# Queries of heads 4 to 7 and probabilities of heads 0 to 3 turned by VectorE blocks and a DRAM scratch, in a two-layer attention and retention trunk

## What is computed

```python
h = rms_norm(x, norm_mix_g[0])
q, k, v = split(h @ a_w_qkv, 3)                      # 256 x 1024 each, 8 heads of 128
q = rope(rms_norm(q per head, q_gain)); k = rope(rms_norm(k per head, k_gain))
s = q @ k.T * 128 ** -0.5;  s = where(causal, s, -1e30);  p = softmax(s)
x = x + (p @ v) @ a_w_o
x = x + square(relu(rms_norm(x) @ w1)) @ w2          # layer 0's MLP
x = x + retention_mixer(rms_norm(x));  x = x + mlp(rms_norm(x))
```

## Time and profile before

| | us |
|---|---|
| median of 3 runs | 663.09 (661.23 to 663.13) |
| the profiled execution's own time | 662.9 |
| its span, first to last instruction | 661.1 |
| PE busy | 655.7 (99% of the span) |
| DVE busy | 430.3 (65%) |
| ACT busy | 332.4 (50%) |
| POOL busy | 26.8 (4%) |

### The profile page before, as it was taken

How to read it: one execution, slowest core, us unless ns; L and a number is a source line. 1 busy time by engine, 2 the same in 40 slices (tenths; PEclk the granted TensorE clock), 3 DMA queues, 4 the chain that set the end, 5 groups by cost and what they waited for, 6 DMA issues and landing times.

```text
span 661.1 us, 8673 instructions
## 1 busy us (share of the span) xinstructions
PE 655.7 (99%) x3248; PEld 553.4 (84%) x3248; DVE 430.3 (65%) x481; ACT 332.4 (50%) x435; POOL 26.8 (4%) x29
## 2 busy tenths in 40 slices
PE   8999999999999999999999999999999999999998
PEld 7888888888888888888888888888888888888887
DVE  6798656877776445549984765765588777744531
ACT  7777664655554333454445555554465555533320
POOL 0163000000000000000000000000000000000000
PEclk9999999999999999999999999999999999999999
DMA  9965457766555657554655657649847655565500
GB/s 325 389 220 190 128 152 246 202 188 188 187 189 192 192 192 257 194 183 154 225 192 193 191 161 276 197 149 288 234 148 216 193 193 183 191 208 195 187 1 32
DMA packets 90766, 129.30 MB, mean 196 GB/s; under 512 B 3312, under 2 KB 50928, under 8 KB 90736
## 3 DMA queue, kind: packets, MB, share of 16 engines
q1 hardware_dynamic: 90448, 127.58, 59.6%
q0 software_dynamic: 288, 1.31, 0.5%
HBM read 124.68 MB, written 4.19 MB: 195 GB/s over the span
## 4 chain that ended last, share of the span: by engine, by line
PE 99%; DVE 0%; issue 0%; DVEq 0%
PE acc L635 23%; PE acc L539 19%; PE acc L541 19%; PE acc L540 19%; PE acc L638 11%; PE acc L586 1%; PE acc L583 1%; PE acc L592 1%; PE acc L658 1%; PE scr L541 1%; PE scr L540 1%; PE scr L539 1%; PE scr L671 1%; PE scr L682 1%; PE scr L703 1%; PE scr L766 1%
## 5 line engine op out<-in xcount | busy, mean ns | idle before, releaser
L1046 DVE TENSOR_TENSOR lo<-raw,hi 128x2048 fp32r<-128x2048 f32 x108 | 247.1, 2288 | 109.6 <-ACT hi L806 109.5
L806 ACT ACTIVATE hi<-raw 128x2048 fp32r<-128x2048 f32 x108 | 207.0, 1918 | 139.4 <-PE acc L541 137.4
L635 PE MATMUL acc<-h_both,hi 128*128 128x512 f32 x640 | 224.0, 396 | 0.0
L638 PE MATMUL acc<-h_both,lo 128*128 128x256 f32 x640 | 178.3, 279 | 0.0
L635 PEld LDWEIGHTS acc<-h_both,hi 128*128 128x128 f32 x640 | 120.1, 188 | 28.5
L638 PEld LDWEIGHTS acc<-h_both,lo 128*128 128x128 f32 x640 | 120.5, 188 | 0.0
L539 PE MATMUL acc<-hi,aT_hi 128*128 128x512 f32 x252 | 98.1, 389 | 0.0
L541 PE MATMUL acc<-hi,aT_lo 128*128 128x512 f32 x252 | 98.0, 389 | 0.0
L540 PE MATMUL acc<-lo,aT_hi 128*128 128x512 f32 x252 | 98.0, 389 | 0.0
L539 PE MATMUL acc<-hi,h_both 128*128 128x512 f32 x208 | 83.4, 401 | 0.0
L541 PE MATMUL acc<-hi,h_both 128*128 128x512 f32 x208 | 81.2, 390 | 0.0
(11 more groups left out here) (132 smaller groups left out, 582.5 us busy)
## 6 DMA issues: line engine op xcount, KB each, us to landing
raw<-in_mlp_w SPq DMA_DIRECT2D x64, 1024.0 KB, 5.4
raw<-in_r_w_in SPq DMA_DIRECT2D x24, 1024.0 KB, 5.1
raw<-in_a_w_qkv SPq DMA_DIRECT2D x8, 1024.0 KB, 9.8
raw<-in_r_w_out SPq DMA_DIRECT2D x8, 1024.0 KB, 5.2
raw<-in_a_w_qkv SPq DMA_DIRECT2D x16, 256.0 KB, 6.1
raw<-in_a_w_o SPq DMA_DIRECT2D x4, 1024.0 KB, 5.0
z_rows<-stage_a SPq DMA_DIRECT2D x32, 64.0 KB, 1.8
stage_b<-z_rows SPq DMA_DIRECT2D x8, 256.0 KB, 2.8
```

The lines of the kernel that those rows point to most:

```text
L635: nc.tensor.matmul(bank, feat_view(hi, s)[:, kt, o * P:(o + 1) * P], h_both[:, kt, :, :].rearrange("p b t -> p (b t)"), start=kt == 0, sto ...
L638: m = nc.tensor.matmul(bank[:, 0:SEQ], feat_view(lo, s)[:, kt, o * P:(o + 1) * P], hT_hi[:, kt, :], start=False, stop=kt == KD - 1)
L806: nc.scalar.activation(hi[:, s, :], raw[:, s, :], ACT.Copy).then_inc(hi_ready, 1)
L1046: nc.vector.tensor_tensor(lo[:, s, :], raw[:, s, :], hi[:, s, :].bitcast(F32), ALU.subtract).then_inc(lo_ready, 1)
```

## The change

`T` of groups 4 and 5 and `P` of heads 0 to 3 leave PE and ACT. In their place DVE turns 32x32 blocks: `turn_queries(4)` and `(5)` as a new task `B` at slot 14, into `q_blocks`, and a transpose of 384 columns at the end of `normalised(h)` for h < 4, into `p_blocks`. SP writes the blocks to the DRAM scratches `q_rows` and `p_rows` (four DMAs for each group or head) and reads them back into `qkT` (four DMAs per group, in runs of 32 elements) and `pT` (one per head). `scores(4)` waits for both query reads, `attend(h)` for h < 4 for its read. Its right operand is then read from `pT` in runs of 32. The low part of chunk 9 moves from slot 14 to 15, and that of chunk 10 from 15 to 17. In slots 10 to 19 `left` and `var` now come before `N`.

```diff
-    early = ["scales", "rope", "high", "low", "N", "v", "raw", "left", "var", "T", "A", "P", "S", "E"]
+    early = ["scales", "rope", "high", "low", "left", "var", "N", "B", "v", "raw", "T", "A", "P", "S", "E"]
...
+TURNED = (4, 5)
+STORED = [p for p in range(8) if p not in TURNED]
+TURN_AT = 14
...
-LOW_AT = {1: 3, 3: 4, 5: 7, 7: 9, 9: 11, 11: 13, 13: 14, 17: 18}
+LOW_AT = {1: 3, 3: 4, 5: 7, 7: 9, 9: 11, 11: 13, 13: 15, 15: 17, 17: 18}
...
-            for s, (n, kg) in enumerate(WO_ORDER):
-                load(C_WO // 4, s, tok_view, wo_w[n, kg])
+
+            def write_queries():
+                for t in range(TT):
+                    sp.wait_ge(q_blocks_ready, t + 1)
+                    for i in range(4):
+                        rows = q_rows[t].rearrange("(j r) i c -> i r j c", j=4)[i]
+                        sp.dma_start(rows, q_blocks[32 * i:32 * i + 32, t, :].rearrange("p (j c) -> p j c", j=4)
+                                     ).then_inc(q_out[t], 16)
+
+            def read_queries():
+                for t in range(TT):
+                    sp.wait_ge(q_out[t], 64)
+                    for a in range(4):
+                        sp.dma_start(qkT[:, 0, 4 + a, t * P:(t + 1) * P].rearrange("p (i c) -> p i c", i=4),
+                                     q_rows[t].rearrange("d i (a c) -> a d i c", a=4)[a]).then_inc(q_in[t], 16)
...
+            def read_probs(h):
+                sp.wait_ge(p_out[h], 64)
+                sp.dma_start(pT[:, h, :], p_rows[h].rearrange("d i c -> d (i c)")).then_inc(p_in[h], 16)
...
+            load_wo(0)
+            write_probs(0)
+            write_queries()
+            read_probs(0)
+            write_probs(1)
+            load_wo(1)
+            read_queries()
+            read_probs(1)
+            load_wo(2)
+            write_probs(2)
+            read_probs(2)
+            write_probs(3)
+            load_wo(3)
+            read_probs(3)
...
             def scores(h):
-                pe.wait_ge(qkT_ready, 4 + 4 * (h // 4))
+                pe.wait_ge(qkT_ready, 4 + 2 * (h // 4))
+                if h == 4:
+                    for t in range(TT):
+                        pe.wait_ge(q_in[t], 64)
...
-                pe.wait_ge(pT_ready, h + 1)
+                if h < 4:
+                    pe.wait_ge(p_in[h], 16)
+                    p = pT[:, h, :].rearrange("p (i b c) -> p b i c", i=4, b=3)
+                    first, second = p[:, 0:2], p[:, 2]
+                else:
+                    pe.wait_ge(pT_ready, h - 3)
+                    first, second = pT[:, h % 4, 0:SEQ], pT[:, h % 4, SEQ:384]
...
-                    if what == "T":
+                    if what == "T" and i in STORED:
                         transpose_rot(i)
...
-                    elif what == "P":
+                    elif what == "P" and i >= 4:
                         transpose_p(i)
...
+            def turn_queries(p_i):
+                t = p_i % 2
+                dve.wait_ge(rot_sum_ready, p_i + 1)
+                nc.vector.transpose(q_blocks[:, t, :].rearrange("p (j a c) -> p a j c", j=4, a=4),
+                                    rot[:, t, :].rearrange("p (a j c) -> p a j c", a=4, j=4)
+                                    ).then_inc(q_blocks_ready, 1)
...
+                if h < 4:
+                    dve.wait_ge(p_ready, h + 1)
+                    if h >= 2:
+                        dve.wait_ge(p_out[h - 2], 64)
+                    nc.vector.transpose(p_blocks[:, h % 2, :].rearrange("p (j b c) -> p b j c", j=4, b=3),
+                                        probs[:, h % 3, :].rearrange("p (b j c) -> p b j c", b=3, j=4)
+                                        ).then_inc(p_blocks_ready, 1)
```

More of the change, by code:

```diff
@@ L126, in attention_schedule @@
         at[O_AT[h]].append(("O", h))
+    for p in TURNED:
+        at[TURN_AT].append(("B", p))
     at[SCALES_AT].append(("scales", 0))
     first = ["T", "square", "var", "rope", "factors", "low", "raw", "high", "left"]
-    early = ["scales", "rope", "high", "low", "N", "v", "raw", "left", "var", "T", "A", "P", "S", "E"]
+    early = ["scales", "rope", "high", "low", "left", "var", "N", "B", "v", "raw", "T", "A", "P", "S", "E"]
     late = ["N", "A", "S", "v", "high", "O", "P", "E", "low"]
@@ L181, in program @@
     x_rows = nc.dram_tensor("x_rows", (2, TT, P, 4, P), F32, kind="Internal").ap()
+    q_rows = nc.dram_tensor("q_rows", (TT, P, 4, P), F32, kind="Internal").ap()
+    p_rows = nc.dram_tensor("p_rows", (4, P, 4, 3 * 32), F32, kind="Internal").ap()
     z_rows = nc.dram_tensor("z_rows", (HR, TT, P, 4, P), F32, kind="Internal").ap()
@@ L242, in program @@
         rope_g = at("rope_g", 55 * KB, [P, 2, TT, 2, P])
+        p_blocks = at("p_blocks", 61 * KB, [P, 2, 384])
         mask = at("mask", 59 * KB, [P, 384])
@@ L297, in program @@
         qkT_ready = sem("qkT_ready")
+        q_blocks_ready = sem("q_blocks_ready")
+        q_out = [sem(f"q_out{t}") for t in range(TT)]
+        q_in = [sem(f"q_in{t}") for t in range(TT)]
         v_ready = sem("v_ready")
@@ L304, in program @@
         pT_ready = sem("pT_ready")
+        p_blocks_ready = sem("p_blocks_ready")
+        p_out = [sem(f"p_out{h}") for h in range(4)]
+        p_in = [sem(f"p_in{h}") for h in range(4)]
         o_ready = sem("o_ready")
@@ L424, in _, with write_probs, load_wo @@
                 load_qkv(c)
-            for s, (n, kg) in enumerate(WO_ORDER):
-                load(C_WO // 4, s, tok_view, wo_w[n, kg])
+            def write_queries():
[11 more added lines that the diff above has]
+                                     q_rows[t].rearrange("d i (a c) -> a d i c", a=4)[a]).then_inc(q_in[t], 16)
+            def write_probs(h):
+                sp.wait_ge(p_blocks_ready, h + 1)
+                for i in range(4):
+                    rows = p_rows[h].rearrange("(j r) i c -> i r j c", j=4)[i]
+                    sp.dma_start(rows, p_blocks[32 * i:32 * i + 32, h % 2, :].rearrange("p (j c) -> p j c", j=4)
+                                 ).then_inc(p_out[h], 16)
+            def read_probs(h):
+                sp.wait_ge(p_out[h], 64)
+                sp.dma_start(pT[:, h, :], p_rows[h].rearrange("d i c -> d (i c)")).then_inc(p_in[h], 16)
+            def load_wo(s):
+                load(C_WO // 4, s, tok_view, wo_w[WO_ORDER[s]])
+            load_wo(0)
[12 more added lines that the diff above has]
+            read_probs(3)
             load_w1(0)
@@ L668, in transpose_rot @@
                 if p_i >= 1:
-                    pe.wait_ge(qkT_ready, p_i)
+                    pe.wait_ge(qkT_ready, STORED.index(p_i))
                 for h in range(4):
@@ L686, in transpose_p @@
                 pe.wait_ge(p_ready, h + 1)
-                if h >= 1:
-                    pe.wait_ge(pT_ready, h)
+                if h >= 5:
+                    pe.wait_ge(pT_ready, h - 4)
                 b = scr[:, 1, :]
@@ L702, in attend @@
                 bank = scr[:, BANK_O[h % 2], :]
-                nc.tensor.matmul(bank[:, 0:SEQ], v_att[:, 0, h * P:(h + 1) * P], pT[:, h % 4, 0:SEQ],
+                nc.tensor.matmul(bank[:, 0:SEQ], v_att[:, 0, h * P:(h + 1) * P], first,
                                  start=True, stop=False)
-                nc.tensor.matmul(bank[:, P:SEQ], v_att[:, 1, h * P:(h + 1) * P],
-                                 pT[:, h % 4, SEQ:384], start=False, stop=True).then_inc(o_ready, 1)
+                nc.tensor.matmul(bank[:, P:SEQ], v_att[:, 1, h * P:(h + 1) * P], second,
+                                 start=False, stop=True).then_inc(o_ready, 1)
             def behind(k):
                 for what, i in SCHEDULE[k]:
-                    if what == "T":
+                    if what == "T" and i in STORED:
                         transpose_rot(i)
@@ L898, in store_pT @@
             def store_pT(h):
-                act.wait_ge(pTp_ready, h + 1)
-                if h >= 4:
-                    act.wait_ge(o_ready, h - 3)
+                act.wait_ge(pTp_ready, h - 3)
+                act.wait_ge(o_ready, h - 3)
                 nc.scalar.copy(pT[:, h % 4, :], scr[:, 1, 0:384]).then_inc(pT_ready, 1)
@@ L917, in _ @@
                         norm_squares(0)
-                    elif what == "T":
+                    elif what == "T" and i in STORED:
                         store_qkT(i)
@@ L1145, in rope @@
                     dve.wait_ge(tables_g_ready, 2)
-                if p_i >= 2:
-                    dve.wait_ge(rotT_ready, p_i - 1)
+                if p_i - 2 in TURNED:
+                    dve.wait_ge(q_blocks_ready, p_i - 2 - TURNED[0] + 1)
+                elif p_i >= 2:
+                    dve.wait_ge(rotT_ready, STORED.index(p_i - 2) + 1)
                 sin_done = dv.mark(nc.vector.tensor_tensor(u4, raw4, sin, ALU.mult))
@@ L1179, in masked @@
                 dve.wait_ge(pow_ready, POWER_NO[4 * (h // 4) + 1])
-                if h >= 3:
-                    dve.wait_ge(pTp_ready, h - 2)
+                if 3 <= h < 7:
```

(5 more changed lines are left out.)

5 lines of the change are left out of this document (3 added, 2 removed).

## The result

The changed kernel takes 667.36 us (median of 10 runs, 665.58 to 671.15) against 663.33 for the kernel before beside it: a ratio of 1.0066, 95% interval 1.0049 to 1.0084. It is slower, by some 4.4 us as the ratio has it and 4.0 between the medians, where 1.5 had been forecast. The profiled execution took 669.16 us, its span is 667.4. The trace of after starts 0.25 us later in the work than that of before (the DVE step behind `low` 8 starts at 48.28 and 48.53), so 0.25, its shift, is added to its times where they are set against before's.

What follows compares the result with a forecast made beforehand. PE was taken to bound the kernel, 99% of the chain. 2.20 us won against 3.9 in waits for POOL gave +1.66 on the profiled 662.9, so 664.6 us; range 661.8 to 667.2.

Steps and rivals of the forecast that it cites:

- The ledger of DVE: DVE from `low` 8's end at 48.53: transposes at 0.61 each put `var` 6 at 61.42, `low` 10 at 62.82.
- The collisions: POOL products and DVE steps exclude each other; group 6's meets `low` 10 at 62.8, group 7's meets `low` 11.
- The sum for POOL's wait: PE at `T` 7: starts at 70.1 for 68.11, +2.0 us; less 0.33 for `P` 3, +1.66 to the end.
- scratch trips on SP: SP's DRAM writes and reads, costed at nothing; head 3's read lands at 79 to 80, `attend(3)` asks at 82.1.
- The sign that I had set for it: The forecast is wrong in the step if PE waits at `S` 4 or `attend`.
- the margin as the thinnest of all: Head 3's probability read before `attend(3)` asks for it: 2 us to spare.
- Rival 4: PE after the 3 us wait: TensorE at 1.2 GHz, some 25 matmuls 0.2 slower each, half counted: 667; chance 0.10.
- Short runs in `attend`: PE's right operand in runs of 32: between no cost and 2.6 us over four heads, taken as none.
- Rival 3: Query reads land late, 77.3 against 73.9 when `S` 4 asks, +3.4 us on top: 668; chance 0.08.
- Rivals 1 and 2: 1: PE does not wait, -2.2, 660.9, chance 0.10; 2: DVE's ledger too long, 662 to 663.4, chance 0.14.

Runs made afterwards that it cites:

- the run with both edits: Changed kernel with head 3's read ahead of the fourth output projection load and twelve unused matmuls ahead of the wait at `T` 6: 664.73 us, ratio 1.0031.
- holding the clock: Changed kernel with twelve matmuls whose result nobody reads ahead of the wait at `T` 6: 666.76 us, ratio 1.0062.
- the placed kernel: Changed kernel with `var` 7 a slot sooner, `low` 10, `low` 11 and the high part of chunk 11 a slot later: 667.94 us, ratio 1.0067.
- the last experiment: Changed kernel, `var` 7 sooner, `low` 10, 11 and high 11, 12 later, SP's head 2, 3 writes and reads before both loads: 661.39 us, ratio 1.0002.
- the probabilities alone: Changed kernel with only the probabilities of heads 0 to 3 turned by DVE, queries left on PE: 664.01 us, ratio 1.0016.
- the first run with SP's order mended: Changed kernel, `var` 7 sooner, `low` 10, 11 and high 11, 12 later, reads of heads 2, 3 each ahead of one load: 664.38 us, ratio 1.0024.

## Why the prediction was wrong

- **The ledger of DVE was right.** The wait for head 1's exponential was forecast as 0.9, and is 1.04. `rope` 6 was forecast at 54.49, `var` 6 at 61.42, `low` 10 at 62.82: they are, with the shift, at 54.54, 61.46 and 62.87. The transposes take 0.50 to 0.60 by distance of starts (52.60 to 53.10, and 53.10 to 54.29 for two). The collisions came as worked out, with `low` 10 and the product starting 0.02 us apart. The product for group 7 was to end at 70.0 to 70.1; it ends at 69.89. That the engines take turns so is also the rule of the Trainium skill (SBUF — State Buffer, SBUF: two separate sides, on the shared port pair: whichever starts first has it for the whole instruction). The rows agree that a product and a `low` don't share; which of them goes first the recorded starts don't tell, since the product that starts 0.02 ahead of `low` 10 is the one that waits.
- **The sum for POOL's wait was right to half a microsecond.** With the clock full and the late read out of the way (the run with both edits) `T` 7 starts at 69.90 + 0.50 = 70.4, for 70.1. The rest is a wait that I did not list: `T` 7 needs the copy of `T` 6, and ACT makes the high part of chunk 12 first.
- **The step that failed is "scratch trips on SP", costed at nothing.** I had head 3's read land at 79 to 80, 2 us before `attend(3)` would ask. It landed at 84.7. Three sizes were wrong in it. The query reads, in runs of 128 bytes, take 7.19 us to issue, 0.9 each, where I took 0.44 from the issues of z; that puts the third load at 68.33, for some 64, and head 2's writes right behind it, at 68.80. Those writes landed so late behind it that the next read was issued at 74.62, for 72. And head 3's own read, behind the fourth load, took 6.6 to land, where I took 2.8. The sign that I had set for it, a PE wait at `attend`, is there. Reordering alone (the read ahead of the load) brings the ratio from 1.0066 to 1.0026. Among runs with the full clock only, that is 666.9 (two runs) against 664.5 (eight): 2.4 us. I had named the margin as the thinnest of all and still gave the case in which it fails no chance of its own.
- **Rival 4 happened, and mostly beside the point.** The clock fell after the 2.75 us wait. It moved `T` 7 from 70.40 to 72.11, 1.7 us, where I had 2.5 by estimate. But PE had then less to wait at `attend(3)`, and holding the clock brings only 0.0004 of the ratio (1.0066 to 1.0062, less than the intervals). Without the late read it may show: 1.0 us between the means of the four runs with 0.997 and the eight with 1.0, less than their spread, and 2.7 between two and nine in the placed kernel; holding the clock there (1.0031 against 1.0026) shows nothing. My remark that no wait of before is long enough to show it holds. The Trainium skill (TensorE: Matmul & The Clock Gate, HAM oscillation) has waits between groups of matmuls lower the clock; the traces here agree after waits of 2.0 us and more, though not in every run.
- **Short runs in `attend`** were rightly put at nothing: its 128x256 matmuls take 0.59 for two before (71.63) and after (75.07), and `attend(0)` 0.65 from its first start to the next task's in both.
- **Rival 3** was the right kind of cause in the wrong place: the query reads came in time, those of the probabilities didn't. **Rivals 1 and 2** are out.
- **Why nothing is won even when it is mended.** Of the 2.20 us taken from PE, the last experiment gives back 0.7 of idle time at `T` 6 and 0.2 at L751, and is 0.65 ahead at the end of attention. The rest, some 0.65 (0.16 of it because a wait also loses the overlap of two matmuls), I have not placed.

What stays open is a part of the profiled spans. From the end of attention on, every trace here is the same to 0.1 us but for PE's three stretches of matmuls that read `h_both` (L635 before, L692 after): each runs at one of two paces, from its first to its last start 88.48 or 90.18 us for the two long ones, 44.11 or 44.95 for the short one, without a wait or a lower clock. The group's row in before, in after and in the last experiment:

```profile
L635 PE MATMUL acc<-h_both,hi 128*128 128x512 f32 x640 | 224.0, 396 | 0.0
```

```profile
L692 PE MATMUL acc<-h_both,hi 128*128 128x512 f32 x640 | 225.7, 398 | 0.0
```

```profile
L692 PE MATMUL acc<-h_both,hi 128*128 128x512 f32 x640 | 224.8, 397 | 0.0
```

Of the 6.3 us between the two profiled spans 1.7 are this: before has one slow stretch (1.7), after has two (3.4), the last experiment 2.55. Whether the pace belongs to the program or to the execution the runs don't tell. The ratios above agree, within their intervals, with the lateness at the end of attention alone, but for one: with each read ahead of one load the trace is 2.8 us late, 0.42%, and the interval ends at 0.37%. That trace is of one of the seven runs of twelve in which the clock fell.

## What to carry to other kernels

A trip through DRAM is priced by its place in the issuing engine's program: what is issued just behind a large load lands with it, and a read that waits for such a write holds up everything behind it. Put small, urgent writes and reads ahead of large loads, and price the issue of a new pattern from a row with runs as short, or from both ends. Where two lateness terms meet at one instruction, mending the earlier one shows nothing while the later one stands: the clock held, or DVE placed to spare POOL, left the ratio at 1.0062 and 1.0067, and the placement brought it to 1.0020 only with the read mended. Undo the later one before the earlier is called free.

## What the runs showed that I had not expected

- Issuing a read of 64 KB in runs of 128 bytes took 0.62 to 1.97 us on SP, 7.19 for eight; the writes of the same blocks, in runs of 512 bytes, took 0.46 each (3.70 for eight). The issue right behind the eight, in long runs, took 0.62 too.
- A 192 KB read issued right behind a 1 MB load landed after 6.6 us (5.0 with the probabilities alone); ahead of it, after 2.5 to 2.8. The writes behind a load landed up to 5.5 us after their issue (the first run with SP's order mended), for 1.7 at best.
- TensorE fell to 1.2 GHz in or right after waits of 2.0, 2.3 and 2.75 us in three traces, and kept 2.4 GHz through one of 2.7 in a fourth; by the mean clock the same kernel has runs of both kinds. With two waits of 1.6 us it kept 2.4 GHz in 10 of 11 runs.
